# A two-block transformer kernel on one core: the first expert rows picked by zero-one products, four more filler products, and the scatter products put into the next expert step

## Chip, core and metric

The kernel runs as one program on one core of a Trainium2 chip. The metric is the device time of one execution in microseconds (us), median of several executions; lower is better.

## What is computed

Two transformer stacks follow each other, each of two layers, in float32. The change touches only the mixture of experts of the second stack, which stands once in each of its two layers (272 tokens of 1024 features, 32 experts in 4 groups, 2 experts for each token):

```
hid = silu(einsum('td,edf->tef', t, w1)) * einsum('td,edf->tef', t, w3)
y   = einsum('tef,efd->td', hid * combine[..., None], w2)
```

`combine` is zero but for the two experts that the token chose, so a kernel may compute each expert for its own tokens alone. An expert has a hidden width of 256, so its three weight matrices have 1 MB each, 96 MB in a layer.

## The kernel before

**The expert loop.** In each layer the 32 experts are taken in 8 groups of 4. One step of the loop (`expert_step`) handles one group with up to 32 tokens for each of its 4 experts, 128 slots in all; a group whose busiest expert has more than 32 tokens takes several steps. The number of steps is computed on the chip: both layers take 12. TensorE, VectorE, ScalarE and GpSimd each run a loop over the same steps, held together by semaphores.

**One step on TensorE (PE), in program order.** 64 products of the chosen rows `x_g` with the w1 and w3 weights (L1742, "up"), then four transposes that turn the first half of the next step's rows (`turn_rows(0)`, L1721), a wait for the hidden values (ScalarE takes the silu, VectorE the product, L2990), two transposes of these (L1753), four more row transposes, 16 products with w2 ("down", L1764), three small products that tell which token sits in which slot of the step after next (`slots`, L1714), 16 more down products, and then `add_out` twice: 24 products with a zero-one matrix `scatter` that add the step's results (`e_out` and its rounding rest `e_rest`, called z_gate in the trace) to the five PSUM banks of the output (L1775, L1777). The `scatter` matrix of the step is written by VectorE (L2987) while the up products run.

**Rows of the next step.** The tokens of a step are fetched by GpSimd with an indirect DMA from a copy of the activations in HBM, `h_rows`, into the one buffer `x_rows` (called h_area in the trace; `fetch`, L2263 to L2265). The fetch of a step is issued in the step before, once `slots` has told the tokens and `turn_rows(1)` has emptied the buffer.

**Before the loop.** PE turns the activations so that tokens lie on partitions (`h_tok`, also in h_area), runs `hold_clock` (products of ones whose result nobody reads, L1181) while VectorE picks the experts, counts places (L1692, L1695), zeroes the five banks (L1699), waits for VectorE's `sel` (a zero-one matrix of tokens by slots, L2921), runs `slots` for the first step, ten more products of ones, waits for the fetched rows of the first step, turns them (L1721, eight transposes), and runs `slots` for the second step. ScalarE copies the turned rows to `x_g`, and the first up products start.

**Weights.** SyncE (SP) issues the weight loads of 1 MB in the order of use into 22 places. The first 22 loads are issued ahead of the loop. From then on a load waits until the up products (its eight w1 and w3 places) or the down products (its four w2 places) of the last step of a group that held the place have ended (L965, L968).

## Time and profile before

| what | value |
|---|---|
| median of 3 executions | 2168.48 us (2166.6 to 2171.07) |
| the profiled execution's own time | 2163.56 us |
| its span, first to last instruction | 2161.8 us |
| PE busy | 1974.4 us, 91% of the span |
| VectorE, ScalarE, GpSimd busy | 43%, 34%, 32% |
| HBM traffic over the span | 187 GB/s |

The busy share of PE is an average over stages with different limits: in parts of the expert loops the core moves more than 400 GB/s and PE waits for weights, in others the DMA engines are idle. So what the change is worth is to be read at the places where the order of work changes, not from the averages. The chain that ended last runs by share of the span through PE 69%, VectorE 8%, DMA 6%.

### The profile page before, as it was taken

To read this page: it belongs to the slowest core of one execution; us is meant where nothing else is said; L and a number is where in the kernel's file an instruction comes from. 1 tells how busy PE (TensorE), PEld (TensorE's weight loads), DVE (VectorE), ACT (ScalarE), POOL (GpSimd) and SP (SyncE) were. 2 spreads that over 40 slices of the span, in tenths; PEclk is the share of its full clock that TensorE was granted. 3 is DMA by queue.
4 is the path that set the end of the run, shared out by engine and by line. 5 is a ranking of instruction groups with operands and counts; after the bars stand their busy time and mean duration, and the time that the engine had idled before them with its cause. 6 is when DMAs were issued, how large, how long until landed. Compare 5 with 4: busy or idle time off the path is not lost.

```text
span 2161.8 us, 36395 instructions
## 1 busy us (share of the span) xinstructions
PE 1974.4 (91%) x14175; PEld 1579.8 (73%) x14179; DVE 937.3 (43%) x1853; ACT 744.1 (34%) x1189; POOL 698.0 (32%) x558
## 2 busy tenths in 40 slices
PE   7989999999999999999989988759999999789866
PEld 6779899998989999997868764324578687544424
DVE  6561436615543366425765351111347753512212
ACT  5554543445545443422323122112223232222212
POOL 6547648785757748820003000000000030000000
PEclk9999999999999999999999889889999999999988
DMA  7334435553435445553410369999243203688693
GB/s 235 97 115 157 136 118 183 179 185 117 137 117 176 137 137 182 175 155 135 140 75 2 136 273 373 421 420 361 102 143 117 98 1 137 267 365 359 280 420 148
DMA packets 196268, 405.93 MB, mean 188 GB/s; under 512 B 18515, under 2 KB 143846, under 8 KB 171286
## 3 DMA queue, kind: packets, MB, share of 16 engines
q1 hardware_dynamic: 192374, 390.20, 49.4%
q0 software_dynamic: 3744, 13.63, 1.7%
q8 instruction: 106, 1.74, 0.3%
q14 instruction: 44, 0.36, 0.1%
HBM read 400.53 MB, written 3.28 MB: 187 GB/s over the span
## 4 chain that ended last, share of the span: by engine, by line
PE 69%; DVE 8%; DMA 6%; ACT 5%; SPq 4%; issue 2%; DVEq 2%; POOL 2%; ACTq 1%; POOLq 0%
PE ps L1021 9%; PE ps L1022 9%; PE ps L1023 9%; PE ps L1360 9%; PE ps L1742 7%; SPq L933 4%; PE ps L1639 3%; PE ps L1764 3%; DMA last_pair<-in_w 2%; POOL weight_ring L2241 2%; DVEq L2284 2%; DMA weight_ring<-in_w 1%; DMA spare<-in_w 1%; PE ps L1095 1%; PE ps L1775 1%
## 5 line engine op out<-in xcount | busy, mean ns | idle before, releaser
L2241 POOL TENSOR_TENSOR weight_ring<-weight_ring 128x512 fp32r<-128x512 f32 (+1 forms) x466 | 628.8, 1384 | 310.5 <-ACT weight_ring L1839 292.8
L1021 PE MATMUL ps<-weight_ring 128*128 128x256 f32 x1824 | 530.2, 291 | 11.0 <-DVE acts L2358 5.0
L1023 PE MATMUL ps<-weight_ring 128*128 128x256 f32 x1568 | 440.5, 281 | 0.0
L1022 PE MATMUL ps<-acts,weight_ring 128*128 128x256 f32 x1472 | 415.9, 283 | 0.0
L1021 PEld LDWEIGHTS ps<-weight_ring 128*128 128x128 f32 x1824 | 346.8, 190 | 23.6 <-issue 22.7
L1023 PEld LDWEIGHTS ps<-weight_ring 128*128 128x128 f32 x1568 | 299.1, 191 | 0.0
L1022 PEld LDWEIGHTS ps<-acts,weight_ring 128*128 128x128 f32 x1472 | 279.8, 190 | 1.9 <-issue 1.4
L1839 ACT ACTIVATE weight_ring<-weight_ring 128x2048 fp32r<-128x2048 f32 x128 | 238.8, 1883 | 92.0 <-PE ps L1023 82.8
L1360 PE MATMUL ps<-acts,weight_ring 128*128 128x272 f32 x896 | 211.1, 394 | 2.8 <-ACTq L2188 1.4
L2263 POOL CAST row_of<-slot_token 128x1 uint32 (+1 forms) x26 | 4.8, 186 | 624.6 <-DVE slot_token L2930 624.6
L1360 PEld LDWEIGHTS ps<-acts,weight_ring 128*128 128x128 f32 x896 | 169.3, 190 | 40.3 <-issue 2.4
L2257 POOL TENSOR_TENSOR acts<-work,tables 128x512 f32<-128x512 f32 (+1 forms) x36 | 38.5, 1090 | 446.8 <-DVE work L2730 392.1
L1742 PE MATMUL ps<-weight_ring,x_g 128*32 128x512 f32 x816 | 138.0, 662 | 33.6 <-DMA last_pair<-in_w 25.0
L1742 PE MATMUL ps<-acts,x_g 128*32 128x512 f32 x320 | 100.0, 627 | 26.6 <-DMA spare<-in_w 12.8
L2990 DVE SCALAR_TENSOR_TENSOR score<-score,slot_gate,ps 128x256 f32<-128x256 f32 x24 | 11.6, 482 | 239.5 <-ACT score L2217 239.5
L2313 DVE TENSOR_TENSOR weight_ring<-weight_ring 128x512 fp32r<-128x512 f32 (+1 forms) x62 | 86.0, 1419 | 64.9 <-ACT weight_ring L1839 64.9
L2217 ACT ACTIVATE score<-ps 128x256 f32<-128x256 f32 x24 | 9.2, 384 | 284.9 <-PE ps L1742 284.9
L1742 PEld LDWEIGHTS ps<-weight_ring,x_g 128*32 128x32 f32 x816 | 34.9, 120 | 90.2 <-issue 88.9
L1022 PE MATMUL ps<-qkv,weight_ring 128*128 128x256 f32 x352 | 99.6, 283 | 0.0
L1742 PE MATMUL ps<-spare,x_g 128*32 128x512 f32 x176 | 85.8, 645 | 0.0
L2998 DVE TENSOR_TENSOR z_gate<-ps,e_out 128x512 fp32r<-128x512 f32 x48 | 33.2, 692 | 119.7 <-ACT e_out L2223 119.7
L1742 PE MATMUL ps<-h_area,x_g 128*32 128x512 f32 x144 | 68.9, 635 | 14.1 <-DMA weight_ring<-in_w 14.1
(482 smaller groups left out, 3706.3 us busy)
## 6 DMA issues: line engine op xcount, KB each, us to landing
weight_ring<-in_w SPq DMA_DIRECT2D x112, 1024.0 KB, 20.2
weight_ring<-in_w_gate_up SPq DMA_DIRECT2D x44, 1024.0 KB, 5.1
weight_ring<-in_w_in SPq DMA_DIRECT2D x16, 2048.0 KB, 8.8
acts<-in_w SPq DMA_DIRECT2D x32, 1024.0 KB, 24.5
weight_ring<-in_x_wkv SPq DMA_DIRECT2D x16, 1024.0 KB, 5.5
weight_ring<-in_w_down SPq DMA_DIRECT2D x16, 1024.0 KB, 5.2
spare<-in_w SPq DMA_DIRECT2D x16, 1024.0 KB
h_area<-in_w SPq DMA_DIRECT2D x16, 1024.0 KB
```

The source lines that it names most:

```text
L933: sp.dma_start(expert_weights(g, m), src).then_inc(expert_in[pair_of(g, m)], 16)
L1021: nc.tensor.matmul(o, wh, xh, start=start, stop=False)
L1022: nc.tensor.matmul(o, wh, xr, start=False, stop=False)
L1023: return nc.tensor.matmul(o, wr, xh, start=False, stop=stop)
L1360: last = nc.tensor.matmul(ps[:, b, 0:S2], ring[:, slot, at + k * step:at + k * step + P], hT[:, k, :], start=(k == 0), stop=(k == KT - 1))
L1639: last = nc.tensor.matmul(ps[:, b, 0:S2], ring[:, s, at:at + P], oT[:, k, :], start=(k == 4), stop=(k == 3))
L1742: last = nc.tensor.matmul(ps[32 * j:32 * j + 32, b, :].rearrange("p (a n) -> p a n", a=2), x_g[:, k, 32 * j:32 * j + 32], expert_weights(g ...
L1764: last = nc.tensor.matmul(ps[32 * j:32 * j + 32, b, :], e_hidT[:, f, 32 * j:32 * j + 32], expert_weights(g, 8 + j)[:, at:at + 512], start= ...
L1839: nc.scalar.activation(r12(high[:, n % HIGH, 0:w]), raw[:, n % RAW, 0:w], ACT.Copy).then_inc(high_ready, 1)
L2241: nc.gpsimd.tensor_tensor(r12(w), w, r12(high[:, n % HIGH, part]).bitcast(F32), ALU.subtract).then_inc(rest_ready, 1)
L2284: nc.vector.drain()
L2313: nc.vector.tensor_tensor(r12(w), w, r12(high[:, n % HIGH, 3 * k * 64:4 * k * 64]).bitcast(F32), ALU.subtract).then_inc(rest_ready4, 1)
```

## The change

Three things are changed, in both layers. First, the rows of the first step are no longer fetched by DMA and turned: `gather_rows` multiplies `h_tok` with `sel`, 24 products of 128 by 128, which gives the chosen rows already turned. The ten products of ones go, the fetch of the first step goes, VectorE's selection for the second step waits until the 24 products have read `sel`, and the load of weight (1, 4), which lies over `h_tok`, waits for them too. Second, there are nine products of ones and not five in the wait for the chosen experts. Third, the scatter products of a step are issued in the step after it: its first half between the up products and `turn_rows(0)`, its second half between the transposes of the hidden values and `turn_rows(1)`. The first step of a layer adds zeros, and a pair of `add_out` behind the loop adds the last step's results. VectorE writes the scatter matrix later in the step.

```diff
@@ SyncE
                     expert_load(1, 3)
                     expert_load(1, 9)
-                    sp.wait_ge(rows_out, 48 * (l + 1))
-                    expert_load(1, 4)
                     b, u = tiles[("rk", l)]
                     sp.wait_ge(full[b], u)
                     expert_load(1, 0)
+                    start = 0 if l == 0 else sp.value_load(steps[0:1, 0, 8:9], min_val=1, max_val=MAX_STEPS // 2)
+                    sp.wait_ge(rows_out, 48 * (l + 1))
+                    sp.wait_ge(loop_full[ROWS[1]], row_use(start, l, 0))
+                    expert_load(1, 4)
@@ TensorE, ahead of the loop
-                hold_clock(begin("rk", l), 5)
+                hold_clock(begin("rk", l), 9)
...
+                def gather_rows(a, before):
+
+                    b = begin_l(ROWS[a], before)
+                    for k in range(4):
+                        at = (4 * a + k) * P
+                        for n, (t0, L) in enumerate(TOK):
+                            last = nc.tensor.matmul(ps[:, b, k * P:(k + 1) * P], h_tok[0:L, n, at:at + P], sel[0:L, n, :],
+                                                    start=(n == 0), stop=(n == 2))
+                    last.then_inc(loop_full[b], 1)
+
+                pe.wait_ge(htok_ready, 6 * (l + 1))
                 pe.wait_ge(sel_ready, start + (2 * l + 1))
                 slots(start, up_use(start, l, -2))
-                hold_clock(begin_l(ROWS[0], row_use(start, l, -1)), 10)
-                pe.wait_ge(rows_in, start * 16 + 16 * (l + 1))
                 for a in range(2):
-                    turn_rows(a, row_use(start, l, -1))
+                    gather_rows(a, row_use(start, l, -1))
@@ TensorE, expert_step
-                    pe.wait_ge(rows_in, s * 16 + 16 * (l + 2))
+                    pe.wait_ge(scatter_ready, s + (l + 1))
+                    pe.wait_ge(eout_ready, s * 2 + (l + 1))
+                    add_out(0)
+                    pe.wait_ge(rows_in, s * 16 + 16)
                     turn_rows(0, row_use(s, l, 0))
...
+                    add_out(4).then_inc(y_done, 1)
                     turn_rows(1, row_use(s, l, 0))
...
-                    pe.wait_ge(scatter_ready, s + 1)
-                    pe.wait_ge(eout_ready, s * 2 + 1)
-                    add_out(0)
-                    pe.wait_ge(eout_ready, s * 2 + 2)
-                    add_out(4).then_inc(y_done, 1)
@@ TensorE, behind the loop
+                pe.wait_ge(scatter_ready, hi + (l + 1))
+                pe.wait_ge(eout_ready, hi * 2 + l)
+                add_out(0)
+                pe.wait_ge(eout_ready, hi * 2 + (l + 1))
+                add_out(4)
@@ GpSimd
                 pool.wait_ge(rows_out, 48 * (l + 1))
-                fetch(start)
                 pool.wait_ge(loop_full[ROWS[1]], row_use(start, l, 0))
                 fetch(start + 1)
@@ VectorE
+                dve.wait_ge(loop_full[ROWS[1]], row_use(start, l, 0))
                 select_at(start + 1)
                 slots_out(start + 1, up_use(start, l, 0))
                 stop = dve.value_load(steps[0:1, l, 8:9], min_val=1, max_val=MAX_STEPS - 3)
+                nc.vector.tensor_scalar(r12(scatter[:, :]), tok_iota[:, 0:S2], -1.0, None, ALU.is_equal).then_inc(scatter_ready, 1)
+                none = zeros_b[:, :].unsqueeze(1).broadcast_to([P, 2, BANK_W])
+                nc.vector.tensor_copy(r12(e_out[:, :]).rearrange("p (a n) -> p a n", a=2), none)
+                nc.vector.tensor_copy(r12(e_rest).rearrange("p (a n) -> p a n", a=2), none).then_inc(eout_ready, 1)
...
-                    dve.wait_ge(y_done, s + (2 * l + 1))
-                    nc.vector.tensor_scalar(r12(scatter[:, :]), tok_iota[:, 0:S2], slot_token[:, bass.ds(s, 1)], None, ALU.is_equal)\
-                        .then_inc(scatter_ready, 1)
...
                         if a == 0:
                             slots_out(s + 2, up_use(s, l, 3))
+                            dve.wait_ge(y_done, s + (2 * l + 2))
+                            nc.vector.tensor_scalar(r12(scatter[:, :]), tok_iota[:, 0:S2], slot_token[:, bass.ds(s, 1)], None, ALU.is_equal)\
+                                .then_inc(scatter_ready, 1)
```

Where the order moves, the instruction lists show it. On PE ahead of the first loop, the kernel before has, from the zeroing of the last bank to the second `slots` (a semaphore in brackets is waited for; rows_in is the landing of a fetch, loop_free0 to 2 are the banks of the loop coming free):

```order
L1699 MATMUL ps<-zeros_b 128x512 [waits psum_free7]
L1714 MATMUL ps<-slot_cols,sel 128x5 [waits sel_ready,psum_free2,loop_free0,psum_free1,psum_free0]
L1714 MATMUL ps<-slot_cols,sel 128x5 x2
L1181 MATMUL ps<-tables,ones 128x256 [waits loop_free1]
L1181 MATMUL ps<-tables,ones 128x256 x9
L1721 MATMUL ps<-tables,h_area 128x128 [waits loop_free1,rows_in]
L1721 MATMUL ps<-tables,h_area 128x128 x3
L1721 MATMUL ps<-tables,h_area 128x128 [waits loop_free2]
L1721 MATMUL ps<-tables,h_area 128x128 x3
L1714 MATMUL ps<-slot_cols,sel 128x5 [waits loop_free0,sel_ready]
L1714 MATMUL ps<-slot_cols,sel 128x5 x2
```

The changed kernel has at the same place on PE (its lines are two to three higher):

```order
L1701 MATMUL ps<-zeros_b 128x512 [waits psum_free7]
L1716 MATMUL ps<-slot_cols,sel 128x5 [waits htok_ready,sel_ready,psum_free2,loop_free0,psum_free1,psum_free0]
L1716 MATMUL ps<-slot_cols,sel 128x5 x2
L1732 MATMUL ps<-sel,h_area 128x128 [waits loop_free1]
L1732 MATMUL ps<-sel,h_area 128x128 x11
L1732 MATMUL ps<-sel,h_area 128x128 [waits loop_free2]
L1732 MATMUL ps<-sel,h_area 128x128 x11
L1716 MATMUL ps<-slot_cols,sel 128x5 [waits loop_free0,sel_ready]
L1716 MATMUL ps<-slot_cols,sel 128x5 x2
```

The wait for rows_in and the products of ones are gone; 24 products read `sel` and `h_tok` in their place. The wait for sel_ready on the second `slots` is now one that cannot have ended earlier, as VectorE's list shows. Before, ahead of its loop:

```order
L2969 TENSOR_SCALAR pass_at<-pass_at 128x53
L2976 TENSOR_LOAD step_group [waits steps_ready]
L2976 ISA x2
L2919 ISA
L2919 COPY slot_cols<-comb 128x3x4
```

Changed, at the same place on VectorE (loop_full2 is the second bank of gathered rows being complete):

```order
L2982 TENSOR_SCALAR pass_at<-pass_at 128x53
L2989 TENSOR_LOAD step_group [waits loop_full2,steps_ready]
L2989 ISA x2
L2932 ISA
L2932 COPY slot_cols<-comb 128x3x4
```

The selection for the second step moved from beside PE's filler products to behind PE's last gathering product. The third place is inside a step, on PE, behind the up products. Before:

```order
L1742 MATMUL ps<-weight_ring,x_g 32x512 x15
L1748 ISA
L1721 MATMUL ps<-tables,h_area 128x128 [waits loop_free1,rows_in]
L1721 MATMUL ps<-tables,h_area 128x128 x3
L1750 REGISTER_ALU
L1707 REGISTER_ALU [waits ehid_ready]
L1753 MATMUL ps<-tables,score 128x128 [waits loop_free0]
```

Changed, at the same place on PE, with eight of the twelve scatter products between left out:

```order
L1763 MATMUL ps<-weight_ring,x_g 32x512 x15
L1769 REGISTER_ALU
L1749 MATMUL ps<-scatter,e_out 128x272 [waits eout_ready,scatter_ready]
L1751 MATMUL ps<-scatter,z_gate 128x272
...
L1749 MATMUL ps<-scatter,e_out 128x64
L1751 MATMUL ps<-scatter,z_gate 128x64
L1772 ISA
L1723 MATMUL ps<-tables,h_area 128x128 [waits loop_free1,rows_in]
L1723 MATMUL ps<-tables,h_area 128x128 x3
L1709 REGISTER_ALU [waits ehid_ready]
L1777 MATMUL ps<-tables,score 128x128 [waits loop_free0]
```

Twelve scatter products of the step before now stand ahead of the wait for the fetched rows; the other twelve stand behind the two transposes of L1777, and none is left behind the down products.

## Rows read from the trace of the kernel before

**Rows 1.** First line of the profile's page.

```profile
span 2161.8 us, 36395 instructions
```

**Rows 2.** Timeline of PE ahead of layer 0's loop: start, duration, instruction, [idle before, releaser].

```profile
1269.44 2.32 PE L1181 MATMUL ps<-tables,ones 128*128 128x256 f32 x10
1273.68 0.41 PE L1692 MATMUL ps<-chosen,tables 128*128 128x32 f32 x2 [1.91 <-DVEq L2890]
...
1278.45 1.50 PE L1714 MATMUL ps<-slot_cols,sel 128*128 128x5 f32 x6 [0.44 <-DVEq L2925]
1279.88 7.62 PE L1181 MATMUL ps<-tables,ones 128*128 128x256 f32 x20
1290.63 1.09 PE L1721 MATMUL ps<-tables,h_area 128*128 128x128 f32 x8 [3.12 <-DMA h_area<-h_rows,row_of]
...
1292.81 8.77 PE L1742 MATMUL ps<-weight_ring,x_g 128*32 128x512 f32 x64 [0.44 <-DVEq L2932]
```

**Rows 3.** The same stretch as a window: length, busy times, PEclk (granted clock), DMA share, GB/s.

```profile
1275.90:1286.10 10.20, 9.56 (x25) 6.84 (x25) 6.89 (x31) 0.00 (x0) 1.74 (x2) 0.50 1.01 382
```

**Rows 4.** Timeline of PE ahead of layer 1's loop.

```profile
1876.13 6.27 PE L1181 MATMUL ps<-tables,ones 128*128 128x256 f32 x20
1885.65 1.09 PE L1721 MATMUL ps<-tables,h_area 128*128 128x128 f32 x8 [3.25 <-DMA h_area<-h_rows,row_of]
...
1888.26 9.71 PE L1742 MATMUL ps<-weight_ring,x_g 128*32 128x512 f32 x64 [0.52 <-DVEq L2932]
```

**Rows 5.** Timeline of VectorE: the selection for layer 0's second step.

```profile
1286.01 0.17 DVE L2919 COPY slot_cols<-comb 128x12 f32 x1 [1.19 <-issue]
1286.14 0.88 DVE L2921 SCALAR_TENSOR_TENSOR sel<-tables,pass_at,rank 128x128 f32<-128x128 f32 x3
```

**Rows 6.** PE groups by form, 1560 to 1870 us: products of 128 by 128.

```profile
L1588 PE MATMUL ps<-weight_ring,yT 128*128 128x128 f32 x96 | 12.6, 276 | 0.0
```

**Rows 7.** Timeline of PE: scatter products of layer 0's first step, then steps of layer 1.

```profile
1308.44 0.39 PE L1775 MATMUL ps<-scatter,e_out 128*128 128x272 f32 x1
...
1311.28 0.28 PE L1777 MATMUL ps<-scatter,z_gate 128*128 128x128 f32 x1
...
1928.31 8.47 PE L1742 MATMUL ps<-weight_ring,x_g 128*32 128x512 f32 x64 [2.77 <-DMA weight_ring<-in_w]
...
1946.82 7.07 PE L1742 MATMUL ps<-weight_ring,x_g 128*32 128x512 f32 x64
1953.83 0.66 PE L1721 MATMUL ps<-tables,h_area 128*128 128x128 f32 x4
...
2116.58 1.06 PE L1742 MATMUL ps<-acts,x_g 128*32 128x512 f32 x1 [12.73 <-DMA weight_ring<-in_w]
```

**Rows 8.** Who PE waited for from 1270 us on: total us, times, longest.

```profile
PE ps L1753 <- DVEq L2994: 14.4, 24, 0.6
...
PE ps L1764 <- ACT acts L2204: 5.3, 23, 0.3
```

**Rows 9.** A fetch in layer 1, its landing, and the landings of all fetches (issue to landing).

```profile
1944.17 0.95 POOL L2265 DMA_INDIRECT h_area<-h_rows,row_of  x1 [0.84 <-issue]
...
DMA to landing us min/median/max: 9.1/9.1/9.1
...
DMA to landing us min/median/max: 4.0/8.7/10.2
```

**Rows 10.** A window of layer 0's loop, columns as in the window above.

```profile
1390.50:1500.00 109.50, 82.03 (x656) 38.13 (x660) 18.07 (x55) 22.21 (x35) 5.69 (x10) 0.89 1.01 419
```

**Rows 11.** Timeline of SP's queue: where the weight stream starts in layer 0 and restarts in layer 1.

```profile
1301.64 9.93 SPq L933 DMA_DIRECT2D weight_ring<-in_w  x12
...
2022.42 0.80 SPq L933 DMA_DIRECT2D acts<-in_w  x2
```

**Rows 12.** The chain that ended last, two of its pieces: start, duration, what.

```profile
1459.48 9.12 PE ps L1742 x64
...
1547.01 1.04 PE ps L1795 x4
```

More of the change, by code:

```diff
@@ L1732, in _, with add_out @@
                 pe.wait_ge(steps_ready, l + 1)
+                def add_out(i0):
+                    for i, t0, t1, b, at in Y_PIECES:
+                        if i0 <= i < i0 + 4:
+                            nc.tensor.matmul(ps[:, b, at:at + t1 - t0], r12(e_out[:, i * P:(i + 1) * P]), r12(scatter[:, t0:t1]),
+                                             start=False, stop=False)
+                            last = nc.tensor.matmul(ps[:, b, at:at + t1 - t0], r12(e_rest[:, i * P:(i + 1) * P]), r12(scatter[:, t0:t1]),
+                                                    start=False, stop=False)
+                    return last
                 def expert_step(s, g):
```

8 lines of the change are left out of this document (removed).

## The prediction

> **What bounds the kernel now.** I read the page first, then the timeline of PE around both expert loops, the waits of PE, SP's queue, and windows with clock and DMA share. The span is 2161.8 us [rows 1]; only the two expert stages of some 270 us each are touched.
>
> Ahead of each loop the end is set by a chain PE, GpSimd, DMA, PE. In layer 0 `slots` starts at 1278.45, products of ones fill from 1279.88 to 1287.50, then PE idles 3.12 us until the fetched rows land, turns them, and the first up products run from 1292.81 to 1301.58 [rows 2]. The moment they end matters more than anything else there: at 1301.64 SP starts twelve weight loads [rows 11], and from there to 1500 the DMA engines are never idle (share 1.01 at 419 GB/s from 1390.5 on) [rows 10]. Every group whose start waits for weights is therefore pinned to that moment. The last one so pinned in layer 0 starts at 1459.48; from there five steps run back to back on PE until the banks are closed at 1547.01 [rows 12].
>
> In layer 1 the order is mixed. The third group starts at 1928.31 when its weights come [rows 7], and then seven steps run without a weight wait. The groups have many steps here, so places come free late and the stream runs dry; it restarts at 2022.42, at the end of the sixth of these steps' up products [rows 11]. The last three groups are pinned to that restart, the last starting at 2116.58 after 12.73 us of waiting [rows 7]. So on the path stand: the head, five whole steps and one run of up products, and after the weights have come one whole step.
>
> **The four more products of ones.** Ten records (five products) of 256 columns took 2.32 us [rows 2], so four more take 1.86. The wait they stand in is 1.91 us in layer 0 [rows 2]. They end 0.05 us before the chosen experts are known: no cost in time. What covers them is VectorE's choice; without it they would cost 1.86 a layer. What they may give is clock: in layer 0 the granted clock is 0.50 from 1275.9 to 1286.1, that is 1.2 GHz, behind this idle time [rows 3].
>
> **The gathered rows.** Added are 24 products of 128 by 128 a layer, two records each. 96 such records keep PE 12.6 us [rows 6], 0.131 each, so 48 take 6.3 us at full clock. At half clock I bound them by the ones: 20 records of 256 columns took 7.62 us when mostly at half clock [rows 2], and twice the warm time is 12.6. Removed are the filler products, the idle 3.12, and eight transposes of 1.09 us. New is what VectorE does behind them. Before, its selection (L2919, L2921) ended at 1287.02 [rows 5], hidden under the wait for the rows. Now it cannot start until the last gathering product has ended. A load of a register and its issue took 1.19 us ahead of L2919, with two drains in it; I take 1.0. The selection takes 1.01 (1286.01 to 1287.02), its signal 0.3, `slots` 0.8 at full clock, and then 0.43 as before until the up products, with 0.3 more because PE's own two register loads are now exposed behind the late `slots`. That is 3.9 us from the last gathering product to the first up product. Before, 1.09 us passed there (1291.72 to 1292.81).
>
> Layer 0, clock high throughout: slots 1278.45 to 1279.2, gathering to 1285.5, first up product 1289.4 instead of 1292.81: 3.4 us won. If the clock stays low until 1286.1 as it did [rows 3], PE has done some 23 records by then (6.15 us by 0.262), the other 25 take it to 1289.4, and a start at 1293.3 is no gain. Layer 1: slots ended at 1876.13 [rows 4], gathering to 1882.4, start 1886.3 instead of 1888.26: 2.0 us won, or 0.4 when the gathering loses as much to the half clock as the fillers there did (6.27 us for 20 records against 4.64, twice the 2.32 of full clock). The up products then took 8.77 and 9.71 us [rows 2, 4] against 7.07 at full clock [rows 7]. Some of this half-clock time, 1.7 and 2.6 us, may come back, but the new idle time of 2.3 us behind the gathering makes it likely that PE starts low again; I take 0.8 us won over both layers. I take 3.0 for layer 0 (the ones fill the idle time that stood ahead of the low clock), 1.3 for layer 1, and 0.8: **head 5.1 us**, with 0 and 10 as ends.
>
> Every pinned start moves with it: SP's stream starts earlier by the same amount, since each of its later loads waits for PE events that move too. Load (1, 4) now waits for the gathering, some 10 us later than before, on idle DMA engines and 20 us ahead of its group: nothing. VectorE's zeroing (one scatter matrix, two copies of 1024 columns) lies under the first up products: nothing.
>
> **The scatter products.** They take 3.12 us a step (1308.44 to 1311.56) [rows 7]. Inside a step PE idles 0.60 us for the hidden values, 24 times 14.4 us in all, and 0.23 for their copy, 5.3 in 23 times [rows 8]. The twelve products behind the up products (about 1.55 us) cover the first, the other twelve the second. That is 0.83 us for each step on the path. On it are five steps in layer 0, and five and one in layer 1: 11 x 0.83 = 9.1 us won. But the sum has another side: in before, each pinned group's predecessor did its scatter products in the wait for weights, for nothing. Now they stand in the pinned step, and the loop is followed by one more `add_out` pair. In both layers the last stretch holds one pair more than before: 2 x 3.1 = **6.2 us lost** (in layer 1 the middle stretch holds five pairs before and five after).
>
> **The fetched rows of the next step.** Moving twelve scatter products of the whole 24 behind the up products brings `turn_rows(0)` closer to the fetch. Before, in a back-to-back step, the fetch was issued at 1944.17, landed 9.1 us later at 1953.27, and was used at 1953.83 [rows 7, 9]: 0.56 us to spare. Now `turn_rows(0)` comes about 1.55 us earlier: PE waits 1.0 us there. With the median landing of 8.7 it waits 0.6, with the longest, 10.2, it waits 2.1, and with the shortest, 4.0 us, when the weight stream is dry, nothing [rows 9]. Of the eight such uses on the path four fall where the stream runs; four at 0.7 are **2.8 us lost**.
>
> The Trainium skill (DMA: Bandwidth & Descriptors, "Anatomy of one DMA — SWDGE (gpsimd) path") fits a DMA issued by GpSimd at about 2.0 us plus its bytes at 436 GB/s. For the 0.5 MB of a fetch that would be an estimate of 3.2 us, so by the page no step would wait for its rows, and the sum would be 2.8 us better. The measured landings of 8.7 in the median speak against it, and the sum goes by them.
>
> **The sum.** 5.1 + 9.1 - 6.2 - 2.8 = 5.2 us less. Against the profiled execution's own 2163.56 that is 2158.4 (its span is 1.76 shorter than its time). That execution lies 4.9 below the median of the runs, so I put the difference on the median: 2168.48 - 5.2 = 2163.3.
>
> **The rivals.**
>
> *One wait for another (B).* PE's wait for the fetch is replaced by a gathering at half clock and the wait for VectorE's selection; the head gives 0 to 1 us. For it: the clock was at half in the gathering's place in both layers [rows 3, 4]. Against it: the longer fillers. Sum 0.5 + 0.1 = 0.6 us less, 2167.9.
>
> *More than forecast (C).* The clock stays high through the gathering and the first up products and fetches land sooner since they are alone in the head: 3.4 + 2.0 in the start, 1.7 + 2.6 in the up products, and half of the fetch waits gone: 9.7 + 0.1 + 1.4 = 11.2 us less, 2157.3. The Trainium skill (TensorE: Matmul & The Clock Gate, "Part 4: PE-mode transpose") says that transposes do not count as activity for the clock as products do; the change puts products where eight transposes stood. No row here separates the two. Against this rival: 2.3 us of idle time ahead of the first up products remain.
>
> *Late rows (E), the other side.* The fetch becomes what each back-to-back step waits for, also where the stream was dry before, since faster steps and a stream closer to them make landings longer. At 10.2 us in all eight uses the waits are 8 x 2.0 = 16 us instead of 2.8, and the sum is 8.0 us more, 2176.5. From a mean wait of 1.0 us over the eight uses on the kernel is no faster than before, from 1.5 on it is slower by more than 0.2%. For it: only 0.56 us to spare before. Against it: landings of 4.0 in dry stretches, with 2 of layer 0's four uses there.
>
> *No effect (D).* The weights bound both loops and the head is absorbed: a start of the stream that moves 5 us earlier brings weights 5 us earlier only if HBM and the queues keep their pace. Against it: the share is 1.01 throughout. 2168.
>
> **How the numbers follow.** Forecast 0.45, B 0.20, C 0.15, D 0.08, E 0.12. The forecast's own range, from the ends of head and fetch waits, is 2160 to 2166.5. B, C and D lie inside 2157 to 2170, E outside; so this range leaves out about 0.15 with the tail of C. A measurement of this kernel tells about 0.2%, 4.3 us, from no change, so faster means below 2164.1: two thirds of the forecast (0.30), all of C (0.15), a little of the rest: 0.48. Slower means above 2172.8: most of E, 0.11. The same: 0.41.
>
> **What the profile after would show.** Right: 48 records of the gathering in 6 to 9 us, first up products of layer 0 near 1289 to 1290 and of layer 1 near 1886; L2919's successor about 1.0 us behind the last gathering product; no idle time in front of the hidden values' transposes; back-to-back steps shorter by up to 0.8 us; PE waiting for h_area in the loop where no such wait stood; a scatter pair of 3.1 us behind each loop; SP's first twelve loads earlier by the head's gain. Wrong: a gathering of 10 us or more, up products as long as before, PE waits for h_area of 2 us in every step, or a stream that starts earlier and delivers at the old time.

## The result, and the profile after

| what | before | after |
|---|---|---|
| median of the executions compared on one chip | 2166.65 us (20) | 2172.36 us (20) |
| range | 2160.83 to 2173.8 | 2168.89 to 2179.88 |
| the profiled execution's span | 2161.8 us | 2171.9 us |

The ratio is 1.0029, 95% interval 1.002 to 1.0039. The changed kernel is slower by 5.7 us in the median, and by 10.1 us between the two profiled executions. Forecast were 5.2 us less. Of all the executions in this document two, both of e10, took far longer than their neighbours (2399.2 and 9435.21 us) and are left out of its median.

First the page's head and the timeline of PE ahead of layer 0's loop, then that ahead of layer 1's loop; they answer to [rows 1, 2, 4].

```profile
span 2171.9 us, 36611 instructions
```

```profile
1270.05 4.05 PE L1183 MATMUL ps<-tables,ones 128*128 128x256 f32 x18
1274.29 0.41 PE L1694 MATMUL ps<-chosen,tables 128*128 128x32 f32 x2 [0.18 <-DVEq L2903]
...
1279.05 0.89 PE L1716 MATMUL ps<-slot_cols,sel 128*128 128x5 f32 x6 [1.45 <-DVEq L2938]
1279.87 14.38 PE L1732 MATMUL ps<-sel,h_area 128*128 128x128 f32 x48
1296.45 1.53 PE L1716 MATMUL ps<-slot_cols,sel 128*128 128x5 f32 x6 [2.20 <-DVEq L2938]
1298.50 8.39 PE L1763 MATMUL ps<-weight_ring,x_g 128*32 128x512 f32 x64 [0.52 <-DVEq L2945]
...
1878.87 15.06 PE L1732 MATMUL ps<-sel,h_area 128*128 128x128 f32 x48
1895.96 1.53 PE L1716 MATMUL ps<-slot_cols,sel 128*128 128x5 f32 x6 [2.03 <-DVEq L2938]
1898.00 9.01 PE L1763 MATMUL ps<-weight_ring,x_g 128*32 128x512 f32 x64 [0.52 <-DVEq L2945]
```

The ones fill their wait (0.18 us of idle time where 1.91 stood). A product takes two records, so the 24 products of the gathering (L1732) are 48 records. They take 14.38 and 15.06 us, where the forecast had 6.3. The wait behind them is there and has its forecast size: from the end of the gathering (1294.25) to the first up product (1298.50) it is 4.25 us, against 3.9 in the prediction. In the windows (length, busy times, granted clock, DMA share, GB/s), which answer to [rows 3], the low level now begins later and does not end within the gathering:

```profile
1278.50:1280.00 1.50, 0.95 (x7) 0.94 (x8) 1.16 (x7) 0.00 (x0) 0.00 (x0) 1.00 0.88 339
1280.00:1286.00 6.00, 6.00 (x23) 4.54 (x23) 3.97 (x16) 0.00 (x0) 0.00 (x0) 0.56 0.98 403
1286.00:1294.00 8.00, 8.00 (x27) 6.16 (x26) 0.00 (x0) 0.60 (x1) 0.00 (x0) 0.50 0.04 15
```

PE is busy for all of 1280 to 1294 and still runs at 0.50, that is 1.2 GHz, for nearly all of it. In layer 1 the clock is at 0.50 from before the gathering to behind its end.

Then the timeline of PE's weight loads (PEld) in the gathering. It shows the pattern of the products, four records with 128 rows of weights and two with 16, and a gap at each change of the number of rows:

```profile
1281.07 0.93 PEld L1732 LDWEIGHTS ps<-sel,h_area 128*128 128x128 f32 x4 [0.22 <-issue]
1282.22 0.50 PEld L1732 LDWEIGHTS ps<-sel,h_area 16*128 16x128 f32 x2 [0.22 <-issue]
1282.94 0.93 PEld L1732 LDWEIGHTS ps<-sel,h_area 128*128 128x128 f32 x4 [0.23 <-issue]
```

One column tile takes 1.87 us (1282.94 less 1281.07), and eight of them make 15.0. Where the number of rows does not change, records of this form start 0.213 us apart at this clock, and 0.111 us apart at full clock (both in the trace of e7, a run further on). Six records would thus take 1.28 us; the two changes in a column tile cost the other 0.59, 0.30 each. A change costs more than its visible gap of 0.22, because the record behind it starts late as well. A layer's gathering has 16 changes: 15 between its products and one at its first product, since the last product of `slots` has 16 rows. Token tile 2 has only 16 tokens; that is where the 16-row products come from.

In the loops, the chain that ended last has a back-to-back step of layer 0 (one that waits for no weights), before and then after (start, duration, what):

```profile
1513.04 7.05 PE ps L1742 x64
...
1529.99 1.40 PE ps L1742 x9
```

```profile
1515.33 6.87 PE ps L1763 x64
...
1530.78 1.27 PE ps L1763 x9
```

From up products to up products it took 16.95 us, and now 15.45: 1.5 us less, not 0.83. A step that begins a new group took 17.56 and takes 15.80. The pair behind the loop stands on the chain as forecast, from 1546.25 until the banks are closed from 1549.35 (in [rows 12] 1547.01):

```profile
1546.25 0.39 PE ps L1749
...
1549.35 1.04 PE ps L1809 x4
```

Last the waits of PE (total us, times, longest). The waits for fetched rows within the loops are new:

```profile
PE ps L1763 <- DMA weight_ring<-in_w: 43.2, 5, 14.3
...
PE ps L1723 <- DMA h_area<-h_rows,row_of: 8.2, 9, 2.4
```

**Where the 10.1 us went.** Work ahead of the heads moves both layers' stages, so I subtract how late the first router product in front of each head is: 0.62 us in layer 0 (1264.04 less 1263.42) and 2.01 in layer 1 (1861.55 less 1859.54; that holds what layer 0 lost).

In layer 0 the first up products end 1306.89 - 1301.58 - 0.62 = 4.7 us later, and the last group pinned to the weights starts 1464.64 - 1459.48 - 0.62 = 4.5 later. Its five steps and the pair win 2.8 of this, so 1.7 us are lost there. In layer 1 the first up products end at 1907.01, not 1897.97: 7.0 later by the same measure. The head thus costs 11.7 us in both layers, where 5.1 were to be won.

In layer 1 the third group starts 7.1 us later (1937.40, before 1928.31), and the weight stream restarts 6.3 later (2030.78, before 2022.42). The five steps between won only 0.7 us, where 1.5 each would be 7.5. One of them, from 1987.47 to 2008.22, took 20.75 us. In it PE waits for late fetched rows; the three lines are from the chain that ended last, PE's timeline, and a window:

```profile
1987.65 10.72 DMA h_area<-h_rows,row_of
```

```profile
1998.41 1.11 PE L1723 MATMUL ps<-tables,h_area 128*128 128x128 f32 x4 [2.36 <-DMA h_area<-h_rows,row_of]
```

```profile
1997.60:2004.30 6.70, 5.89 (x30) 4.90 (x34) 0.00 (x0) 1.58 (x3) 0.00 (x0) 0.50 1.02 427
```

The step is 5.3 us longer than one without such a wait (15.45): 2.36 us of waiting, and the rest in the stretch in which the granted clock fell to 0.50 during that wait. Three more such waits of 0.49 to 0.78 us stand on this chain in steps that no longer wait for weights; these steps took 16.11 us (not 15.45), 16.42 (not 15.45) and 16.74 (not 15.80). Together the late rows cost 7.9 us on the path of this execution. Behind the restart of the stream 1.7 us more are lost, the pair's 3.0 less what one shorter step wins, so the end is 8.1 us later.

### The profile page after: what moved, and what is told of

The parts are those of the page before. It is cut to its first block, busy times and chain, and to the rows that moved or that the text cites. A ratio compares the mean times of both kernels' runs of the same rounds, so it can differ in the third digit from the quotient of the medians.

```text
span 2171.9 us, 36611 instructions
## 1 busy us (share of the span) xinstructions
PE 1986.4 (91%) x14279; PEld 1596.2 (73%) x14283; DVE 941.0 (43%) x1859; ACT 744.1 (34%) x1189; POOL 696.0 (32%) x554
## 4 chain that ended last, share of the span: by engine, by line
PE 68%; DMA 9%; DVE 8%; ACT 5%; SPq 3%; DVEq 2%; issue 2%; POOL 2%; ACTq 1%; POOLq 0%
PE ps L1023 9%; PE ps L1024 9%; PE ps L1025 9%; PE ps L1362 9%; PE ps L1763 5%; DMA weight_ring<-in_w 3%; SPq L933 3%; PE ps L1641 3%; DMA h_area<-h_rows,row_of 2%; PE ps L1789 2%; POOL weight_ring L2255 2%; DVEq L2297 2%; PE ps L1732 1%; DMA last_pair<-in_w 1%; DMA spare<-in_w 1%
```

## The experiments

The theory after the comparison: the gathering is the loss, and the scatter products ahead of the transposes are a gain. The rival: late fetched rows (8.2 us of waits) are the loss, and would be with any head. Each run is compared with executions of the kernel before taken together with it; that kernel's median was between 2164.35 and 2166.26 us. The diffs are shortened, with `...` where lines are left out.

### The parts apart

**e1_scatter_ones** is the changed kernel with the head's fetch and transposes back.

```diff
...
+                hold_clock(begin_l(ROWS[0], row_use(start, l, -1)), 10)
+                pe.wait_ge(rows_in, start * 16 + 16 * (l + 1))
...
-                    gather_rows(a, row_use(start, l, -1))
+                    turn_rows(a, row_use(start, l, -1))
...
+                fetch(start)
```

> The changed kernel with its head put back: the first rows are fetched by DMA and turned again behind ten products of ones; the nine products of ones and the moved scatter products stay. Theory 1 (the gathering products are the loss, the scatter part gains): 2 to 7 us less than before, ratio 0.997 to 0.999; back-to-back steps 1.5 us shorter than the 16.95 of before, PE waits for fetched rows in the loop of 0.2 to 2.4 us each; up products of layer 0 start where they did before, near 1293. Theory 2 (the loss is the fetched rows coming late in the loop, my rival E): 3 to 8 us more than before, ratio 1.0015 or more, also without the gathering.

Measured: 2160.75 us (2158.76 to 2164.65, 11 runs), ratio 0.9978 [0.9969, 0.9987]. So the scatter part with the ones wins 4.7 us, though PE waits for fetched rows in the loop nine times with it too, up to 2.3 us. The rival falls as the account of the loss: late rows alone do not make the kernel slower. They still take part of the gain.

**e2_gather_ones** is the kernel before with the gathering and the nine ones; the scatter products stay behind the down products.

```diff
-                hold_clock(begin("rk", l), 5)
+                hold_clock(begin("rk", l), 9)
...
-                hold_clock(begin_l(ROWS[0], row_use(start, l, -1)), 10)
-                pe.wait_ge(rows_in, start * 16 + 16 * (l + 1))
...
-                    turn_rows(a, row_use(start, l, -1))
+                    gather_rows(a, row_use(start, l, -1))
```

> The kernel before with the gathering of the first rows and the nine products of ones, and the scatter products where they were. Theory 1: the 48 records take 14 to 15 us a layer at half clock and the weight stream starts 4.7 and 7 us later: 9 to 13 us more than before, ratio 1.004 to 1.006. Theory 2: no more than 3 us from before, ratio 0.999 to 1.0015.

Measured: 2178.98 us (2176.04 to 2184.1, 6 runs), ratio 1.0064 [1.0046, 1.0081]; the gathering takes 14.29 and 15.06 us. Alone it costs some 14 us. Together with e1's gain that makes +9.2, with 3.3 to 14.7 by the two intervals; the whole change has +5.7.

**e11_ones9_alone** is the kernel before with one number changed, in the wait for the chosen experts.

```diff
-                hold_clock(begin("rk", l), 5)
+                hold_clock(begin("rk", l), 9)
```

> The kernel before with nothing changed but nine products of ones where there were five. Prediction on record: no cost and no gain within 0.2 per cent, since the added 1.0 to 1.2 us of products lie in the wait for the chosen experts: ratio 0.999 to 1.001. If the nine end later than the chosen experts are ready, or the clock at the head stands otherwise, up to 2 us either way, 0.999 to 1.001 too; a ratio beyond 1.001 would put part of the loss on them.

Measured: 2165.59 us (12 runs), ratio 1.0 [0.999, 1.0009]. The four products cost nothing and gain nothing. The trace shows what they do: the zeroing of the banks behind them now runs at full clock, but VectorE's `sel` comes no sooner, so PE's wait for it ahead of `slots` grows from 0.44 us [rows 2] to 1.45 in layer 0. Layer 1 of the kernel before had that wait already, with the clock at 0.50 in the stretch behind it. The line of e11, then that of before:

```profile
1279.44 0.89 PE L1714 MATMUL ps<-slot_cols,sel 128*128 128x5 f32 x6 [1.45 <-DVEq L2925]
```

```profile
1875.29 0.92 PE L1714 MATMUL ps<-slot_cols,sel 128*128 128x5 f32 x6 [1.97 <-DVEq L2925]
```

### Why 48 records take 14 to 15 us

Two theories at first. A: the data, since `sel` is nearly all zeros and the clock does not rise over such products. B: the form, that is the 16-row products and the many changes of weights. Where an experiment below gathers other values, layer 1 may route its tokens otherwise, so the time of its gathering is what counts and not its whole time.

**e3_dense_moving** replaces `sel` as moving operand by ones, so that every row comes out as a sum and not as the chosen one.

```diff
-   matmul(ps[...], h_tok[0:L, n, at:at + P], sel[0:L, n, :], ...)
+   matmul(ps[...], h_tok[0:L, n, at:at + P], ones[0:L, :], ...)
```

> The changed kernel, but the gathering products multiply with a matrix of ones and not with the zero-one matrix sel: same shapes, counts and order, a moving operand without zeros. Left out is the choice of rows in the first step (each slot gets the sum of all tokens), so layer 1 may route differently. Theory A (the clock stays at half because of what the operand holds, nearly all zeros): the clock rises during the gathering, which takes 7 to 10 us a layer. Theory B (it stays at half because of the form: 128 columns behind exposed weight loads, every third pair with 16 rows): 14 to 15 us as in the changed kernel, granted clock 0.50 to its end.

Measured (a single run): 2179.63 us, gathering 15.06 us in both layers, clock 0.50. A falls.

**e4_swapped** makes `sel` the weights and the activations the moving operand, so that the rows arrive unturned.

```diff
-   matmul(ps[...], h_tok[0:L, n, at:at + P], sel[0:L, n, :], ...)
+   matmul(ps[...], sel[0:L, n, :], h_tok[0:L, n, at:at + P], ...)
```

> The changed kernel, but in the gathering products the operands change places: sel is the stationary operand, the activations move. Same shapes and counts; the rows come out in the wrong orientation, so the first step computes on other values and layer 1 may route differently. Theory A in its narrow form (zeros in the moving operand count): 7 to 10 us a layer with the clock rising. If zeros in either operand count, or theory B (form): 14 to 15 us at granted clock 0.50.

Measured (a single run): 2173.86 us, 14.49 and 15.06 us, at 0.50 but for the first records of layer 0. Which operand is sparse plays no part either.

**e6_wide_moving** has six products with 512 moving columns in place of 24 with 128; the rows arrive unturned here too.

```diff
-                    for k in range(4):
-                        at = (4 * a + k) * P
-                        for n, (t0, L) in enumerate(TOK):
-                            last = nc.tensor.matmul(ps[:, b, k * P:(k + 1) * P], h_tok[0:L, n, at:at + P], sel[0:L, n, :],
...
+                    for n, (t0, L) in enumerate(TOK):
+                        last = nc.tensor.matmul(ps[:, b, :], sel[0:L, n, :], h_tok[0:L, n, 512 * a:512 * a + 512],
...
```

> The changed kernel, but the gathering is done as 6 products with sel stationary and 512 columns of the activations moving: the same number of columns in all (24 times 128), a quarter of the weight loads. The rows come out unturned, so the first step computes on other values and layer 1 may route differently. If the form holds the clock down (few columns behind each weight load): it rises to 1.00 within the gathering, 12 records in 6 to 9 us a layer. If only the level at its start counts: half clock to the end, 10.2 us (12 records of 0.85).

Measured (a single run): 2167.08 us, 10.87 and 10.54 us. The same columns with a quarter of the weight loads and 4 changes of rows take some 4 us less. The clock is still at 0.50 from 1281.1 to the end in layer 0, and for the first 9.4 us in layer 1. So it is not the many changes alone that go with the low clock.

**e7_no_16_rows** leaves out the products of token tile 2, so the tokens 256 to 271 are never gathered into the first step.

```diff
-                        for n, (t0, L) in enumerate(TOK):
+                        for n, (t0, L) in enumerate(TOK[0:2]):
...
-                                                    start=(n == 0), stop=(n == 2))
+                                                    start=(n == 0), stop=(n == 1))
```

> The changed kernel without the gathering's third part, the products with 16 rows: 16 products, 32 records a layer. Left out is the share of the last 16 tokens in the first step's rows. If the products with 16 rows hold the clock down: the clock rises within the gathering, 4.5 to 7 us a layer. If all products of this form do: half clock to the end, 32 records of 0.31 = 9.9 us.

Measured (a single run): 2158.69 us. The timeline of PE, and two windows as above:

```profile
1279.53 5.39 PE L1732 MATMUL ps<-sel,h_area 128*128 128x128 f32 x32
```

```profile
1279.50:1282.80 3.30, 3.30 (x16) 3.28 (x17) 2.69 (x11) 0.00 (x0) 0.00 (x0) 0.50 0.99 412
1282.80:1286.80 4.00, 2.12 (x19) 1.93 (x18) 2.20 (x10) 1.42 (x3) 0.00 (x0) 1.00 0.93 332
```

Without them the clock falls behind the same wait and is back 3.3 us after the gathering's start; in layer 1 (5.20 us) it is back after 2.9. A third of the records, and the low clock that goes with them, cost over 60% of the gathering's time. What in the 16-row products keeps the clock low stays open: with them it stayed low behind 16 changes of rows, behind 9 (e9, below) and, for most of the time, behind 4 (e6).

**e5_fill_sel_wait** puts three products of ones in the 1.45 us in which PE waits for VectorE ahead of `slots`.

```diff
                 pe.wait_ge(htok_ready, 6 * (l + 1))
+                hold_clock(begin_l(ROWS[0], row_use(start, l, -1)), 3)
                 pe.wait_ge(sel_ready, start + (2 * l + 1))
```

> The changed kernel with three more products of ones between the zeroing of the banks and the first slots, so that PE does not idle for sel (1.4 us) ahead of the gathering. Theory B1 (the gathering keeps whatever level of the clock it starts at, and the idle wait ahead of it lowers it): the clock stays at 1.00, the 48 records take 6 to 7 us a layer, and the kernel is 12 to 18 us faster than the changed one, ratio to before 0.994 to 0.998. Theory B2 (products of this form lower the clock by themselves): it starts high and falls within the gathering, 11 to 15 us a layer, ratio to before 1.001 to 1.004.

Measured: 2160.66 us (2157.88 to 2162.91, 11 runs), ratio 0.9983 [0.9974, 0.9992]. Its PE timeline, and two windows:

```profile
1277.07 1.56 PE L1183 MATMUL ps<-tables,ones 128*128 128x256 f32 x6
1278.47 0.81 PE L1716 MATMUL ps<-slot_cols,sel 128*128 128x5 f32 x6
1279.21 8.51 PE L1732 MATMUL ps<-sel,h_area 128*128 128x128 f32 x48
1289.93 1.25 PE L1716 MATMUL ps<-slot_cols,sel 128*128 128x5 f32 x6 [2.21 <-DVEq L2939]
```

```profile
1279.20:1287.70 8.50, 8.50 (x49) 6.51 (x48) 4.12 (x16) 0.60 (x1) 0.00 (x0) 1.00 0.76 310
1290.00:1297.00 7.00, 6.11 (x30) 2.30 (x34) 2.75 (x10) 0.65 (x1) 1.72 (x2) 0.52 0.50 189
```

The very same products take 8.51 us, with the clock at 1.00 throughout, in layer 1 too. There the clock had fallen at 1873.9, ahead of the wait, and the ones are the work over which it came back, at 1877.4. So this gathering holds the full level for its 8.5 us when it meets no fall of the clock, and does not get the level back when it meets one. With one line more the change is a gain, 11.7 us less than the changed kernel. That is just short of my 12 to 18. I had also expected 6 to 7 us for the gathering, but the changes of rows cost time at full clock too, (8.51 - 48 x 0.111) / 16 = 0.20 us each. The second window shows the next loss: behind the 2.2 us in which VectorE selects, the up products begin at half clock.

**e9_paired_16** issues the token tiles as 0, 1, 2 and 2, 1, 0 in turn, so that the 16-row products stand in pairs.

```diff
-                        for n, (t0, L) in enumerate(TOK):
+                        order_n = (0, 1, 2) if k % 2 == 0 else (2, 1, 0)
+                        for n in order_n:
...
```

> The changed kernel with the 24 gathering products of a layer in another order: token tiles 0, 1, 2 for one column tile and 2, 1, 0 for the next, so that the eight products with 16 rows of weights stand in four pairs and the number of rows changes 8 times in a layer and not 16. No wait or product is added or left out. Switch (the extra price of the 16-row products is paid where the number of rows changes): of the 4.8 us that they cost beyond 32 x 0.117 at full clock, about half goes; at half clock 14.4 us becomes about 10 to 11, and where the clock then rises within the gathering, less: 8 us a layer or so less over both layers, 2162 to 2167. Own price (a 16-row product costs 0.3 us a record wherever it stands): gathering 14.3 to 15.1 us as before, and the time that of the changed kernel, 2170 to 2173.

Measured: 2170.06 us (10 runs), ratio 1.0013 [1.0002, 1.0024]; gathering 12.32 and 12.98 us, at half clock. The order leaves 9 changes where there were 16 (the one at the first product stays, so it is not half). Seven changes less at 0.30 us are 2.1 us, and 2.06 and 2.08 are measured: the price is the change of rows. Four 16-row records in a row take as long as four with 128 rows (0.93 us above):

```profile
1282.70 0.92 PEld L1734 LDWEIGHTS ps<-sel,h_area 16*128 16x128 f32 x4 [0.22 <-issue]
```

My expectation of 10 to 11 us and of the clock's return was off.

### What then is left to gain

**e8_late_turn** is e1's kernel with `turn_rows(0)` behind the second half of the scatter products; ScalarE copies the hidden values first.

```diff
-                    pe.wait_ge(rows_in, s * 16 + 16 * (l + 2))
-                    turn_rows(0, row_use(s, l, 0))
...
                     add_out(4).then_inc(y_done, 1)
+                    pe.wait_ge(rows_in, s * 16 + 16 * (l + 2))
+                    turn_rows(0, row_use(s, l, 0))
...
```

> The first experiment's kernel (no gathering, scatter products moved) with both turns of the fetched rows behind the second half of the scatter products; ScalarE copies the hidden values first. Theory 1 with the waits for fetched rows as the remaining loss: these waits (0.6 to 2.3 us in nine places, some 6 us of them on the path) go, and PE waits about 0.2 us a step for ScalarE's copy of the rows instead; 2 to 6 us faster than the first experiment, ratio to before 0.995 to 0.997. Rival: the copies of rows come onto PE's path and take it back, a ratio as in the first experiment, 0.998, or above.

Measured: 2156.99 us (6 runs), ratio 0.9972 [0.996, 0.9984]. The waits for fetched rows in the loop are gone but for one of 0.23 us. Against e1's 0.9978 the time is not told apart.

**e10_fill_late** is the changed kernel with e5's three ones and e8's order.

```diff
+                hold_clock(begin_l(ROWS[0], row_use(start, l, -1)), 3)
...
-                    pe.wait_ge(rows_in, s * 16 + 16)
-                    turn_rows(0, row_use(s, l, 0))
...
                     add_out(4).then_inc(y_done, 1)
+                    pe.wait_ge(rows_in, s * 16 + 16)
+                    turn_rows(0, row_use(s, l, 0))
...
```

> The changed kernel with two edits: three 512-column products of ones ahead of the first slots product (gathering then ran at full clock, 8.5 us), and turn_rows(0) of the next step behind the second half of the scatter products, with ScalarE copying the hidden rows ahead of the turned rows. If the two gains add up: the first took the time to a ratio of 0.9983 of the kernel before, and the second took the variant with the fetch-and-turn head from 0.9978 to 0.9972, so 0.0006 or 1.3 us more, or up to the 8.2 us in which the changed kernel waited for fetched rows within its steps: ratio 0.995 to 0.9978, 2154 to 2160. If the second only exchanges one wait for another: 0.998 to 0.9985.

Measured: 2160.57 us (2156.23 to 2168.58, 10 executions), ratio 0.9979 [0.9965, 0.9993], as e5. The waits of PE show an exchange: e5's 6.6 us for rows in eight waits are down to one of 0.6, and there is a new wait for ScalarE at the down products.

```profile
PE ps L1790 <- ACTq L2220: 7.9, 24, 0.4
```

**e12_all_three** adds e9's order to e10. **e13_fill_paired** is e12 without the late turn, here as the diff against e12.

```diff
+                    pe.wait_ge(rows_in, s * 16 + 16)
+                    turn_rows(0, row_use(s, l, 0))
...
                     add_out(4).then_inc(y_done, 1)
-                    pe.wait_ge(rows_in, s * 16 + 16)
-                    turn_rows(0, row_use(s, l, 0))
...
```

> The kernel of e10 with the gathering products in the paired order of e9. Switch: the gathering at full clock falls from 8.5 us to about 6 us, 4 to 5 us over both layers, ratio 0.9955 or less if e10 is at 0.997 to 0.998. Own price: gathering 8.5 us again and the time that of e10.

> The kernel of e12 with turn_rows back ahead of the hidden values' transposes, as the change has it: the changed kernel with three products of ones ahead of slots and the paired order. It waits for fetched rows again (some 7 to 8 us in nine or ten waits), and the 7.9 us of 24 waits for the activation ahead of the down products go. If the late rows cost time on the path that the late turn saves (on record: 2.8 us): ratio 0.0013 or more above e12, 0.9965 or more. If the one wait only takes the place of the other: the ratio of e12, 0.9945 to 0.996; if the activation's waits are the dearer ones, below it.

Measured, e12: 2156.33 us (2154.09 to 2157.74, 6 runs), ratio 0.9952 [0.9939, 0.9965]. The gathering takes 7.17 us in both layers at full clock, 1.34 less than in e5 for seven changes less, 0.19 each; my 6 us had counted too much for a change. e13: 2159.39 us (6 runs), ratio 0.9962 [0.9947, 0.9977], with 7.3 us of waits for rows. The two are not told apart, and the steps of the two traces show why. Apart from the first step behind a wait for weights, a back-to-back step of e12 takes 15.8 to 16.2 us. In e13 one without a wait takes 15.45 (15.80 at a new group), and one with a wait of 0.4 to 1.0 us takes 16.2 to 16.6. From the last pinned group of layer 0 to the last step's up products it is 65.5 us in e12 and 65.0 in e13. So the late turn costs each step some 0.35 us and saves what the late rows cost; what it removes besides is the risk of a wait long enough for the clock to fall, as in the step of 20.75 us of the changed kernel.

```profile
1278.91 0.81 PE L1716 MATMUL ps<-slot_cols,sel 128*128 128x5 f32 x6
1279.66 7.17 PE L1734 MATMUL ps<-sel,h_area 128*128 128x128 f32 x48
1289.03 0.92 PE L1716 MATMUL ps<-slot_cols,sel 128*128 128x5 f32 x6 [2.21 <-DVEq L2941]
1291.08 8.57 PE L1766 MATMUL ps<-weight_ring,x_g 128*32 128x512 f32 x64 [1.13 <-DVEq L2948]
```

**e14_second_sel** gives e12's selection for the second step a place of its own, so VectorE need not wait for the gathering.

```diff
+        sel_b = e_pair[:, 2 * DE - 3 * P:2 * DE].rearrange("p (n c) -> p n c", n=3)
...
-                slots(start + 1, up_use(start, l, -1))
+                slots(start + 1, up_use(start, l, -1), sel_b)
...
-                dve.wait_ge(loop_full[ROWS[1]], row_use(start, l, 0))
-                select_at(start + 1)
+                select_at(start + 1, sel_b)
```

> The kernel of e12 with a buffer of its own for the second step's selection, so that VectorE makes it during the gathering; the wait of VectorE for the last gathering product goes because nothing is overwritten any more. If the selection behind the gathering is on the path (on record: 1.0 + 1.0 + 0.3 us exposed a layer): PE's waits of 2.21 and 2.04 us behind the gathering go, the first up products start 2 us earlier in each layer, and both with the earlier start of the weight stream and the clock that then does not fall there it is 4 to 6 us less than e12, ratio 0.9925 to 0.9935. If another wait takes its place (GpSimd's, the slot's counts or the first weights of the loop): the ratio of e12, 0.9945 to 0.996.

Measured: 2150.3 us (2148.15 to 2150.46, 5 runs), ratio 0.9917 [0.99, 0.9933].

```profile
1278.67 0.82 PE L1717 MATMUL ps<-slot_cols,sel 128*128 128x5 f32 x6
1279.42 7.17 PE L1735 MATMUL ps<-sel,h_area 128*128 128x128 f32 x48
1286.62 0.92 PE L1717 MATMUL ps<-slot_cols,score 128*128 128x5 f32 x6
1288.76 7.07 PE L1767 MATMUL ps<-weight_ring,x_g 128*32 128x512 f32 x64 [1.23 <-DVEq L2949]
...
1877.84 8.77 PE L1767 MATMUL ps<-weight_ring,x_g 128*32 128x512 f32 x64 [1.01 <-DVEq L2949]
```

The 2.21 us behind the gathering are gone, and in layer 0 the up products run at full clock from their first (7.07 us against e12's 8.57). From `slots` to the end of the first up products e12 took 20.74 us in layer 0 and e14 takes 17.16; [rows 2] has 23.1 there. By the medians this version is some 16 us faster than the kernel before (18 by the ratio) and 22 faster than the changed kernel.

## Why the prediction was wrong

- **The four more products of ones**: no cost, right (e11).
- **The gathered rows, the step that failed**: "96 such records keep PE 12.6 us [rows 6], 0.131 each, so 48 take 6.3 us at full clock. At half clock I bound them [...] twice the warm time is 12.6." Measured are 14.38 and 15.06 us. Two things were missing. The first is the mix of shapes: the price came from a group of equal 128-row products, while every third product here has 16 rows of weights, and each of the 16 changes of rows adds 0.20 us at full clock (e5 and e12) and 0.30 at half (e9). So even the best case is 8.5 us (e5), not 6.3, and the worst lies beyond my bound: 48 x 0.213 + 16 x 0.30 = 15.0. The second is the clock: I let the ones hold it, and looked for its fall in the wait that they fill. In layer 0 it fell behind the next wait, the 1.45 us ahead of `slots`, which the ones had themselves made longer (e11). In layer 1 it fell at 1874.6 already, ahead of that wait, behind the small products that follow the chosen experts. In neither layer did it come back within the gathering; e5's three ones in the wait ahead of `slots` gave 1.00 throughout in both. The difference to 6.3 is 8.1 and 8.8 us, 16.9 in both layers. With the -5.1 of the text that gives +11.8, and the trace shows +11.7. The head's miss is these two, though the agreement to 0.1 us is partly luck: the -5.1 was itself an estimate, with 1.1 us taken off for a low clock.
- **The clock over such products**: for the fillers of [rows 2, 4] the level came back within the stretch, and I carried that over with "PE has done some 23 records by then". It did so for the 128-row products alone (e7) and not, within the gathering, with the 16-row products among them (e3, e4, e9).
- **The exposed selection**: 3.9 us forecast, 4.25 and 4.08 measured, right. What I did not price is that it need not be there: e14 is some 6 us faster than e12 by a second place for `sel`.
- **The scatter products**: right in direction, too small. "0.83 us for each step on the path" was only the idle time of the waits; a step became 1.5 us shorter. In PE's timelines of the two steps above, the three groups of transposes between the up and the down products with their waits took 2.34 us before (1519.97 to 1522.31) and 1.19 after (1523.54 to 1524.17 and 1525.59 to 1526.15), and the scatter products 3.12 and 2.84. The 0.82 of idle time is a part of that; the rest I read as work around each wait that PE cannot overlap with its neighbours, which no run measures by itself. With 1.5 the eleven steps give 16.5 us, not 9.1, and the sum of this part 7.5 less, not 0.1 less; e1 measured 4.7 less.
- **The pair behind the loop**: 3.1 us forecast, 3.03 and 3.00 measured, right.
- **The late fetched rows**: 8.2 us in nine waits, up to 2.4 us, as the text described them, and by the measured landings of [rows 9], which it rightly preferred to the estimate of 3.2 us. On the path the text had four waits at 0.7 us, 2.8 in all. Four are there, and three cost 0.7 to 1.0 us each, as forecast. The fourth was 2.36 us long, and the clock fell during it: 5.3 us. So 7.9 us stood on the path of the profiled execution, not 2.8; what a longer wait does to the clock stood in no term of the sum. How often an execution meets such a long wait no run here counts.
- **The rivals**: B named the right mechanism, a gathering at half clock and a wait for VectorE. Its 0 to 1 us for the head came from the bound of 12.6. E (late rows) was the only case on the slower side, and is not the account of the loss: e1 has the waits too and is faster. But of the forecast's miss some 5 us belong to it.

The forecast's -5.2 with +16.9 for the gathering, -7.4 for the steps and +5.1 for the late rows would be +9.4. Between the two profiled executions 10.1 are measured, between the medians 5.7.

The Trainium skill (TensorE: Matmul & The Clock Gate, "LDWEIGHTS (loading the stationary operand)") says that a weight load's time depends on its columns and not on its rows. The trace agrees: four loads in a row took 0.92 us with 16 rows and 0.93 with 128, both at half clock. What cost time here is the change from one to the other, 0.20 us at full clock and 0.30 at half.

## What to carry to other kernels

Price a new run of products by its own mix of shapes: a short last tile in every accumulation costs more by the change of rows than by its work, so put such products next to each other or leave them for one place. Where the clock is at half, look at every wait ahead of a stretch and not only at the one that the change fills; here three products of ones in a wait of 1.45 us were worth more than the whole change had lost. And where an operand's reuse makes another engine wait for the new work, a second buffer belongs to the change.

## What the runs showed of the hardware

- With 16-row and 128-row products in turn the granted clock stayed at 0.50 over 14 to 15 us in which PE was 100% busy; with the 128-row products alone it was at 1.00 again after 2.9 and 3.3 us (e7). When the same mix began at 1.00, with no wait ahead of it, it stayed there for 8.5 us (e5). Whether the moving operand was mostly zeros made no difference (e3).
- Each change between 128 and 16 rows of weights took 0.30 us at half clock and 0.20 at full clock, beside 0.213 and 0.111 us from record to record without a change.
- A wait of 2.36 us in the loop of the changed kernel was followed by a granted clock of 0.50 until 2004.3, and the step was 5.3 us longer than one without a wait; steps with a wait of 0.49 to 0.78 us were 0.7 to 1.0 us longer.
